# Reordering the SSD output matmuls of a hybrid decoder trunk: chunk by chunk over two heads, or head by head

## The reference

```python
y_diag = jnp.einsum("bcghls,bcsghp->bclghp", w_intra, xdt)      # within the chunk
...
y_off = jnp.einsum("bclgn,bcghpn->bclghp", cc, h_prev) * decay_out   # from the state before it
return (y_diag + y_off).reshape(bsz, lp, SSM_HEADS, SSM_HEAD_DIM)
```

## Time and profile before

| | us |
|---|---|
| median of 3 runs | 2426.32 |
| lowest and highest | 2426.28, 2435.31 |
| the profiled execution (one of the three) | 2435.31 |
| its span, first to last instruction | 2433.5 |

### The profile page before, as it was taken

The page is one execution under the profiler, slowest core; times in us unless marked ns, Lnnn a source line. Parts: engine busy times, 40 slices in busy tenths (PEclk is TensorE's granted clock), DMA queues, the critical chain, the costliest instruction groups (busy, mean ns, idle before and its releaser), DMA issues.

```text
span 2433.5 us, 30923 instructions
## 1 busy us (share of the span) xinstructions
PE 2158.6 (89%) x12521; PEld 1828.4 (75%) x12521; DVE 1291.8 (53%) x1519; ACT 1007.0 (41%) x1080; POOL 60.6 (2%) x57
## 2 busy tenths in 40 slices
PE   6994788999989957788989999898998989989897
PEld 4882466888867834677978788797887878888786
DVE  3526321000015352326867778686876868778686
ACT  2222200000003222106656666566665656657565
POOL 1012000000000120000000000000000000000000
PEclk9995589999999965888999999999999999999999
DMA  6441011344434410035979979798897979979796
GB/s 212 167 130 39 1 69 69 138 147 139 149 138 166 130 39 0 1 104 195 352 244 329 333 241 349 244 348 296 294 334 248 339 248 342 349 234 350 236 342 214
DMA packets 362613, 504.90 MB, mean 207 GB/s; under 512 B 7284, under 2 KB 298220, under 8 KB 361972
## 3 DMA queue, kind: packets, MB, share of 16 engines
q1 hardware_dynamic: 360752, 493.58, 60.1%
q0 software_dynamic: 1264, 8.24, 1.0%
q10 hardware_dynamic: 468, 1.10, 0.1%
HBM read 501.51 MB, written 1.10 MB: 207 GB/s over the span
## 4 chain that ended last, share of the span: by engine, by line
PE 72%; DVE 12%; DMA 10%; ACT 3%; issue 2%; SPq 1%; DVEq 0%; ACTq 0%; POOL 0%; POOLq 0%
PE bank L564 11%; PE bank L779 9%; DMA kept<-in_moe_w 9%; PE bank L680 9%; PE bank L758 8%; PE bank L760 7%; PE bank L759 7%; DVE w_low L1390 6%; PE bank L664 5%; PE bank L694 4%; PE bank L632 2%; PE bank L742 2%; ACT w_high L974 2%; PE bank L798 1%; DVE room L1136 1%
## 5 line engine op out<-in xcount | busy, mean ns | idle before, releaser
L1390 DVE TENSOR_TENSOR w_low<-kept,w_high 128x2048 fp32r<-128x2048 f32 x378 | 850.7, 2286 | 46.0 <-ACT w_high L974 44.0
L974 ACT CAST w_high<-kept 128x2048 fp32r<-128x2048 f32 x378 | 707.2, 1909 | 150.0 <-DMA kept<-in_moe_w 149.0
L758 PE MATMUL bank<-w_high,x_high 128*128 128x256 f32 x2016 | 597.6, 296 | 39.8 <-DVE w_low L1390 36.1
L760 PE MATMUL bank<-w_high,x_low 128*128 128x256 f32 x2016 | 574.7, 285 | 0.0
L759 PE MATMUL bank<-w_low,x_high 128*128 128x256 f32 x2016 | 574.2, 285 | 0.0
L758 PEld LDWEIGHTS bank<-w_high,x_high 128*128 128x128 f32 x2016 | 389.4, 193 | 89.9 <-DVE w_low L1390 89.3
L759 PEld LDWEIGHTS bank<-w_low,x_high 128*128 128x128 f32 x2016 | 390.3, 194 | 0.0
L760 PEld LDWEIGHTS bank<-w_high,x_low 128*128 128x128 f32 x2016 | 389.9, 193 | 0.0
L564 PE MATMUL bank<-room,kept 128*128 128x272 f32 (+1 forms) x704 | 169.1, 402 | 13.2 <-DVE room L1136 13.2
L564 PEld LDWEIGHTS bank<-room,kept 128*128 128x128 f32 (+1 forms) x704 | 133.4, 191 | 46.4 <-DVE room L1136 14.0
L779 PE MATMUL bank<-w_high,h_high 128*128 128x512 f32 x504 | 157.7, 394 | 9.1 <-DVE h_low L1395 9.1
(11 more groups left out here) (241 smaller groups left out, 2225.5 us busy)
## 6 DMA issues: line engine op xcount, KB each, us to landing
kept<-in_moe_w SPq DMA_DIRECT2D x378, 1024.0 KB, 7.9
kept<-in_w_in SPq DMA_DIRECT2D x10, 2048.0 KB, 9.6
kept<-in_ffn_w SPq DMA_DIRECT2D x8, 2048.0 KB, 7.8
room<-in_w_in SPq DMA_DIRECT2D x6, 2048.0 KB, 10.8
kept<-in_w_out SPq DMA_DIRECT2D x6, 2048.0 KB, 8.1
room<-in_ffn_w SPq DMA_DIRECT2D x6, 2048.0 KB, 7.8
kept<-in_ffn_w SPq DMA_DIRECT2D x4, 1792.0 KB, 8.1
room<-in_ffn_w SPq DMA_DIRECT2D x4, 1792.0 KB, 8.3
```

Of the source, the lines that this page charges most:

```text
L758: pe.matmul(bk[:, 0:EC], xhi[:, k, :], wh[:, k, :], start=(k == 0), stop=False)
L760: last = pe.matmul(bk[:, 0:EC], xlo[:, k, :], wh[:, k, :], start=False, stop=(k == KD - 1))
L974: nc.scalar.copy(whi[kind][:, c % 2, :], raw_w[kind][:, c % 2, :]).then_inc(hi_ready[kind], 1)
L1390: V.tensor_tensor(out=wlo[kind][:, c % 2, :], in0=raw_w[kind][:, c % 2, :], in1=whi[kind][:, c % 2, :].bitcast(F32), op=ALU.subtract).then ...
```

## The change

Inside a bank, the loops over the chunk and over the two heads change places. Before: for each chunk, the `xdt` product of head 2j, of head 2j+1, then the state product of head 2j, of head 2j+1. After: all five matmuls of head 2j (three chunks), then all five of head 2j+1. The matmuls, their operands, their destinations and flags, the semaphores and the number of instructions are the same.

```diff
-                        for c, (t0, L) in enumerate(CH):
-                            for o in range(2):
-                                h = 2 * j + o
-                                last = pe.matmul(bk[64 * o:64 * o + 64, t0:t0 + L], xdt[0:L, c, h * 64:(h + 1) * 64],
-                                                 Wt[0:L, h, t0:t0 + L], start=True, stop=(c == 0))
-                            for o in range(2):
-                                h = 2 * j + o
+                        for o in range(2):
+                            h = 2 * j + o
+                            for c, (t0, L) in enumerate(CH):
+                                dst = bk[64 * o:64 * o + 64, t0:t0 + L]
+                                last = pe.matmul(dst, xdt[0:L, c, h * 64:(h + 1) * 64], Wt[0:L, h, t0:t0 + L],
+                                                 start=True, stop=(c == 0))
                                 if c:
-                                    last = pe.matmul(bk[64 * o:64 * o + 64, t0:t0 + L],
-                                                     hst[:, c - 1, h * 64:(h + 1) * 64], AB[:, h, t0:t0 + L],
+                                    last = pe.matmul(dst, hst[:, c - 1, h * 64:(h + 1) * 64], AB[:, h, t0:t0 + L],
                                                      start=False, stop=True)
                         ready(last, name)
```

## The result

The changed kernel takes 2457.61 us (median of 4), the kernel before 2426.3: ratio 1.0114, 95% interval 1.0094 to 1.0135, so 23 to 33 us slower. The forecast was slower, at 2493, with a range of 2451 to 2504. The time lies in the range, but near its lower end, which had been set to reach the first rival. The direction held, and so did the doubling of a bank. The excess did not: 31 us by the medians where 66.5 were summed, since the clock did not do what the forecast assumed. The size is that of the first rival, 2456.

What follows compares the result with a forecast made beforehand. The chain was taken as almost all TensorE, with all four blocks on the path. Group 0 +31.2, group 1 +33.1 and L480 +2.2 made +66.5 us; on 2426.3 that gave 2493 us, range 2451 to 2504.

Steps and rivals of the forecast that it cites:

- the first rival: In the four blocks the clock keeps its old pattern: +29.6 us, 2456 us in all; chance 0.30.
- the choice of the clock: In the four blocks, what the doubling costs depends on the granted clock: 14.9 us a block at full clock, 26.8 at half.
- A bank doubles: In `ssd_out`, one head alone takes what a two-head bank took: 1.24 us at full clock, 2.23 at half.
- The bound from `weigh`: Upper bound for one head of a `y` bank: 0.26 us times ten passes, 2.6 us at half clock.
- The second switch is inside the doubling: In each bank, the added change from 128 to 16 partitions and back costs nothing beyond the doubled time.
- All four blocks are paid in full: The blocks of both groups in both layers lie on the path, and neither VectorE nor DMA absorbs the shift.
- The clock falls in group 0: Group 0 blocks run 4.6 us at full clock, the rest at half: 23.0 us against 7.46, +31.2 over two layers.
- The clock does not rise in group 1: Group 1 blocks stay at half clock, 26.8 us each: +15.6 and +17.5, together +33.1 us.
- L480: Its first twelve passes behind group 1 start on a cold clock, for 1.3 and 3.0 us of excess, halved: +2.2 us.
- The arithmetic of the cold blocks: Block times if the clock falls in group 0 and stays low in group 1: 23.0 and 26.8 us.
- the idle time as an objection: `weigh`'s long cold stretch also has idle time, so it is no proof that one-half work keeps the clock down.

Runs made afterwards that it cites:

- Experiments 3 and 4: Kernel before, two banks at a time: neighbouring matmuls to different banks in the same column half, 2469.52 us; or in different halves, 2446.57 us.
- Experiment 9: Kernel before, each bank with both heads' 16-token products first, then eight long passes of one head, then eight of the other: 2438.36 us, ratio 1.0049.
- experiments 1 and 2: Kernel before with head-by-head order only in the blocks of group 0, 2438.15 us, or only in those of group 1, 2439.95 us; ratio 1.0044 each.
- the copy: Kernel before, unchanged, run again for a second profile: 2425.75 us, ratio 0.9986.
- experiment 7: Changed kernel with 64 partitions of each operand in place of 128, half of each sum left out: 2490.58 us, ratio 1.0246 to the kernel before.
- experiment 6: Kernel before with the two heads of `weigh` alternated matmul by matmul instead of head by head: 2408.72 us, ratio 0.9906.
- experiment 5: Kernel before with, per chunk, both products of one head and then both of the other: 2426.73 us, ratio 0.9994.
- the two-bank form: Kernel before with the `y` products issued for two banks at a time, in two head orders: 2469.52 us for one; 2446.57 and, repeated, 2444.09 for the other.

## Why the prediction was right in kind and wrong in size

The step that failed is the choice of the clock: "I assume that this counts as the end of the dense stretch", and "I assume that one half at a time does not raise it". On them the four blocks came to +64.3 of the 66.5 us summed; they measured +27.0, because the clock kept 1.00 in group 0 and still rose in group 1. The step before it, that a bank doubles, held.

- *A bank doubles.* Right: 1.24 us became 2.47, and 12 head times of 1.23 are a block of group 0, 14.7 us. The bound from `weigh` (2.6 us a head at half clock) was not needed. Experiments 3 and 4 show that it is the column halves.
- *The second switch is inside the doubling.* Right for the changed order. Experiment 9 adds that without the switch between heads half of the long passes overlap again.
- *All four blocks are paid in full.* Right: 27.0 us of longer blocks, 27.3 us at the first expert matmul. In experiments 1 and 2 the blocks of one group gave 10.8 and 11.2 us there for 14.6 of longer blocks; most of the rest is the clock elsewhere.
- *The clock falls in group 0* ("I assume that this counts as the end of the dense stretch"): this step failed. It gave +15.6 us a block; the clock stayed at 1.00 and a block cost +7.3. In the two that is 16.6 us of the miss.
- *The clock does not rise in group 1*: this failed too. +33.1 was summed and +12.4 measured, 20.7 us of the miss. The rise came 4.2 and 3.6 us into the blocks. The first rival had put it at 8.34 us in layer 0, where before had it; it came sooner, so layer 0 paid 5.4 and not 7.4. That is partly the chance of one profile: in the copy the same block of before took 9.5 us and not 11.2, and against it layer 0 paid 7.1.
- *L480*: +2.2 summed. It took 3.00 us in layer 0 (before 4.69, the copy 5.79) and 4.42 in layer 1 (before 3.00), -0.3 in all.

The three misses are 16.6, 20.7 and 2.5, together 39.8; 66.5 less these is 26.7, against 27.3 at the first expert matmul. The arithmetic of the cold blocks was sound, as experiment 7 shows, where the clock did what the forecast assumed: 23.1 and 26.3 us against 23.0 and 26.8. What I had taken for the cause was not it. I read `weigh`'s long cold stretch as the effect of working on one column half. But the changed blocks work on one half at a time, and the clock stayed up in two of them and rose in the other two; and with both halves at work in `weigh` (experiment 6) it still stayed at 0.50. `weigh` has 16-partition passes, switches and idle time in it, and the prediction named only the idle time as an objection. Which of these keeps the clock down there is open. The rival that held had been given 0.30, the forecast 0.48.

The blocks' 27 us agree with the ratio (27.7 us). The medians of four runs each differ by 31; both lie in the interval of 23 to 33.

## What to carry to other kernels

Matmuls with 64 stationary columns that write different partition halves ran two at a time here, if they stood near each other in the program: alternating them per matmul or per pair of matmuls made no difference, eight passes apart lost half of the overlap, and a change of the number of partitions between them lost all. Look for such loops written head by head; here the one that was left was worth 0.9%, where this change lost 1.1%. And before pricing work at half clock, find a row in which the very same kind of pass ran at that clock for the reason assumed; where there is none, the clock is a rival and not a term.

## What the hardware did that I had not expected

- TensorE started a float32 matmul of one column half beside an earlier one of the other half although two passes of the earlier head still stood between them in the program (experiment 5). With eight long passes in a row to one half (experiment 9) the other half started when four of them were left, and no sooner.
- The granted clock was 1.00 through the 14.74 us of a block of one-half passes, most of them on 128 partitions; with those passes on 64 partitions (experiment 7) it fell to 0.50 within the block, 4.1 us after its start.
- The expert stage took 1308 us in three profiles of the two-bank form of `ssd_out` and 1288 to 1299 in the profiles of the others, with the same counts of matmuls and weight conversions in it. The cause is open.
